# First attention: the softmax maxima stand ahead of the stick-breaking operations on VectorE

## The chip, the cores and the metric

The kernel runs on one core of one Trainium2 chip. The core has TensorE (PE, matmuls; its weight loads are shown as PEld), VectorE (DVE), ScalarE (ACT), GpSimd (POOL) and SyncE (SP, which here issues the DMAs). Each engine works through its own instructions in order, and they meet through semaphores. The metric is the time of one execution on the device in microseconds, given as the median of several runs; lower is better.

## The reference

Two transformer-like blocks run one behind the other on 256 tokens of width 1024. The first block begins with two kinds of attention side by side, eight heads each, whose results are normalised, joined and multiplied by `w_o`; then come a mixture of experts and the second block. Only the two attentions matter here (queries in blocks of 128):

```python
def stick_breaking_attention(q, k, v):           # width 64 a head
        z = einsum('bhqd,bshd->bhqs', qi, k) * scale
        strict = kpos[None, :] < qpos[:, None]
        log_fail = where(strict, log_sigmoid(-z), 0.0)
        later = cumsum(log_fail, axis=3, reverse=True) - log_fail
        a = where(strict, exp(log_sigmoid(z) + later), 0.0)
        return einsum('bhqs,bshd->bqhd', a, v)
...
def chunk_causal_softmax_attention(q, k, v):     # width 96 a head
        sc = einsum('bhqd,bshd->bhqs', qi, k) * scale
        allowed = kchunk[None, :] <= qchunk[:, None]     # chunks of 64
        p = softmax(where(allowed, sc, -inf), axis=-1)
        return einsum('bhqs,bshd->bqhd', p, v)
```

The softmax needs the maximum of each row of `sc` before its exponentials. The stick-breaking attention needs no maximum, but a softplus of z (an absolute value, an exponential and a logarithm) and a running sum over the keys.

## The kernel before

Head n of the stick-breaking attention and head n of the softmax attention are handled together, as one head n, in a pipeline of 12 rounds. `attention_rounds()` gives for round i the heads at each of five depths: `new` = i, `one` = i - 1, `two_` = i - 2, `three` = i - 3, `four` = i - 4, each only while it names a head from 0 to 7. TensorE, ScalarE and VectorE each walk over these rounds with code of their own, so the order on each engine is the order in which that code is written; no scheduler and no table of costs moves anything. All score tiles are 128 x 384: two blocks of queries against the keys that they may see.

TensorE, in this order in a round: of `three` the transposes of the softmax weights (pT, L914); of `new` the stick-breaking scores z (L893, L894); of `one` the sums over keys t (L900 to L902); of `new` the transposes of q and k (qkT, L929); of `one` the softmax scores s (L935, L936); then the products with the values, of `three` (stick-breaking) and of `four` (softmax) (L906, L907). Round 1 has nine extra matmuls (L841) ahead of t.

ScalarE: of `two_` the exponential of the stick-breaking weights (L1448) and the softmax exponentials with their row sums (L1455, twice), which wait for the negated maxima (semaphore `neg_max`); of `three` the copy of pT out of its bank (L1465); of `new` Abs, Exp and Ln on z (L1472, L1473, L1474) and the copy of qkT (L1477); then every second round copies of finished outputs (L1480, L1486).

VectorE: of `two_` the masked weights (L1999), the reciprocal of the row sums (L2002) and the scaling of the softmax weights (L2004, L2005, semaphore `probs`); of `one` the sum t plus log weight (L2009); of `new` three operations on z, which I call the stick-breaking operations: L2015, which waits for L1474 (semaphore `log_part`), L2017 (semaphore `fails`, for the sums t of the next round) and L2018, the last reader of z; of `one` the softmax maxima: L2022 writes -1e30 over the parts of s that are not allowed, L2023 and L2024 reduce, L2025 scales and raises `neg_max`.

The five products pT, z, t, qkT and s of a round go through four PSUM banks (`psr0` to `psr3`, `NB` = 4) in turn, in that order, by the list `GROUPS`. TensorE may start a product only when the last reader of the fourth product before it has signalled `bank_drained`. So pT waits for the last reader of z of the round before (L2018); z for L2009; t for L1477; qkT for L1455 of the same round; s for L1465 of the same round.

```python
def bank(name):
    b, u = use(g_at[0], NB)
    g_at[0] += 1
    if u:
        pe.wait_ge(bank_drained[b], u)
    return psr[b]
```

Of the kernel before, what the change touches and what calls it, by code (L numbers as in the profile page):

```python
# [29 lines left out]
ALU = mybir.AluOpType  # L30
# [5 lines left out]
AX = mybir.AxisListType  # L36

P = 128
# [7 lines left out]
QKD, NOPE, ROPE = 96, 64, 32  # L46
ATT = 3 * P
# [50 lines left out]
def attention_rounds():  # L98

    for i in range(H1 + 4):  # L100
        yield i, (i if i < H1 else None), (i - 1 if 1 <= i <= H1 else None), (i - 2 if 2 <= i < H1 + 2 else None),\
            (i - 3 if 3 <= i < H1 + 3 else None), (i - 4 if i >= 4 else None)
# [135 lines left out]
def bank_fills(name):  # L238

    n = GROUP_NO[name]  # L240
    return 1 + sum(g not in LAST_TILE for g in GROUPS[n % NB:n:NB])
# [19 lines left out]
def build(nc, d):  # L261

    with ExitStack() as ctx:
        def sb(name, shape, dt=F32):
            return ctx.enter_context(nc.sbuf_tensor(name, shape, dt))

        def sem(name):
            return ctx.enter_context(nc.semaphore(name))
# [31 lines left out]
        stat = sb("stat", [P, 2, 8])  # L300
# [154 lines left out]
        neg_max = sem("neg_max")  # L455
# [36 lines left out]
        def used(eng, n, it=None, per=0):  # L492

            eng.wait_ge(tile_used, at(it, per, split_no, n + 1))
# [30 lines left out]
        def full(eng, name):  # L525

            b = GROUP_NO[name] % NB
            if name in LAST_TILE:
                used(eng, LAST_TILE[name])
            else:  # L530
                eng.wait_ge(bank_full[b], bank_fills(name))
            return psr[b]

        def drains(ins, name):

            return ins.then_inc(bank_drained[GROUP_NO[name] % NB], 1)

        def drained(eng, name):

            b, u = use(GROUP_NO[name], NB)  # L540
            eng.wait_ge(bank_drained[b], u + 1)
# [11 lines left out]
        def sm(b, k):  # L553
            return stat[:, b, k:k + 1]
# [130 lines left out]
        def _(pe):  # L685
# [111 lines left out]
            def split_tokens(tiles, width, blocks):  # L797


                at_k, starts = 0, range(0)  # L800
                for n in tiles:
                    per = SLOT // width
                    if n == tiles[0]:
                        first = {}
                        for q, (out, bank_no, parts, tb) in enumerate(blocks):
                            first.setdefault(bank_no, q * per)
                        starts = first.values()
                    split_product(n, [(out, slice(j * width, (j + 1) * width),
                                       *(x_[:, tb * P:(tb + 1) * P] for x_ in parts(at_k + j)))
                                      for out, _, parts, tb in blocks for j in range(per)],  # L810
                                  starts if n == tiles[0] else (), weights_move=True)
                    at_k += per
# [999 lines left out]
        def _(dve):  # L1812
            V = nc.vector
            st = Steps(dve, dve_step)
            TT, TS, STT = V.tensor_tensor, V.tensor_scalar, V.scalar_tensor_tensor

            def norm(k, n=D, out=None):

                if k >= BY_LOGS:
                    dve.wait_ge(root, k + 1)  # L1820
                    return
                ps = full(dve, ("norm", k))
                if k in IN_BANK:
                    TS(ms[:, :], ps[:, 0:T], 1.0 / n, EPS, ALU.mult, ALU.add).then_inc(mean_made, 1)
                    dve.wait_ge(root, k + 1)
                    V.reciprocal(rinv[:, :], rms[:, :]).then_inc(inverted, 1)
                    dve.wait_ge(inverted, IN_BANK.index(k) + 1)
                    return
                drains(TS(ms[:, :], ps[:, 0:T], 1.0 / n, EPS, ALU.mult, ALU.add), ("norm", k))
                dve.wait_ge(root, k + 1)  # L1830
                st.do(V.reciprocal(rinv[:, :] if out is None else out, rms[:, :]))
# [162 lines left out]
            for i, new, one, two_, three, four in attention_rounds():  # L1994
                if two_ is not None:
                    dve.wait_ge(weights_in, two_ + 1)
                    if two_ >= 2:
                        dve.wait_ge(o_done, two_ - 1)
                    TT(two["pa"][:, two_ % 2, :], two["dd"][:, two_ % 2, :], mask, ALU.mult).then_inc(sb_probs, 1)  # L1999
                    b = two_ % 2  # L2000
                    drained(dve, ("s", two_))
                    st.do(V.reciprocal(stat[:, b, 6:8], stat[:, b, 4:6]))  # L2002
                    e = two["E"][:, b, :]
                    TS(e[:, 0:P], e[:, 0:P], sm(b, 6), None, ALU.mult)  # L2004
                    TS(e[:, P:ATT], e[:, P:ATT], sm(b, 7), None, ALU.mult).then_inc(probs, 1)  # L2005
                if one is not None:
                    ps = full(dve, ("t", one))
                    drained(dve, ("z", one))
                    drains(TT(two["la"][:, one % 2, :], ps[:, 0:ATT], two["dd"][:, one % 2, :], ALU.add), ("t", one))  # L2009
                if new is not None:  # L2010
                    b = new % 2
                    dve.wait_ge(log_part, new + 1)
                    ps = full(dve, ("z", new))
                    sp_ = two["sp"][:, b, :]
                    st.do(STT(out=sp_, in0=ps[:, 0:ATT], scalar=0.0, in1=two["az"][:, b, :],  # L2015
                              op0=ALU.max, op1=ALU.add))
                    TT(two["spm"][:, b, :], sp_, mask, ALU.mult).then_inc(fails, 1)  # L2017
                    drains(TT(two["dd"][:, b, :], ps[:, 0:ATT], sp_, ALU.subtract), ("z", new))  # L2018
                if one is not None:
                    b = one % 2  # L2020
                    ps = full(dve, ("s", one))
                    st.do(V.memset(ps[0:64, 0:ATT].rearrange("p (a c) -> p a c", a=6)[:, 1:6:4, :], -1e30))  # L2022
                    V.reduce_max(sm(b, 0), ps[:, 0:P], AX.X)  # L2023
                    st.do(V.reduce_max(sm(b, 1), ps[:, P:ATT], AX.X))  # L2024
                    TS(stat[:, b, 2:4], stat[:, b, 0:2], -QKD ** -0.5, None, ALU.mult).then_inc(neg_max, 1)  # L2025
            norm(3, 512)
            apply(sbT, mixed[:, 0:4, :], par("sb_out_norm"), 4, normed)
            norm(4, 512)
# [1 line left out]
            for c in range(4):  # L2030
                ps = full(dve, ("wo", c))
# [12 lines left out]
            for c in range(2):  # L2044
                ps = full(dve, ("pq", c))
# [153 lines left out]
            for q in range(4):  # L2199
                ps = full(dve, ("vt", q))  # L2200
# [38 lines left out]
            for i in range(2 * H2 + 1):  # L2239
                if i < 2 * H2:  # L2240
                    b = i % 2
                    for c in range(2):
                        ps = full(dve, ("s2", i, c))
# [3 lines left out]
                if i >= 1:  # L2247
                    n = i - 1
                    b = n % 2
# [13 lines left out]
            for p_ in range(3):  # L2263
                piece = slice(p_ * 512, (p_ + 1) * 512)
                ps = full(dve, ("rt2", p_))
# [3 lines left out]
            for c in range(4):  # L2269
                ps = full(dve, ("eo", c))  # L2270
# [150 lines left out]
            ps = full(dve, ("mean", 0))  # L2421
# [10 lines left out]
            for c in range(4):  # L2432
                ps = full(dve, ("pw2", c))
# [206 lines left out]
```

## Time and profile before

| what | us |
|---|---|
| median of 3 runs | 1791.12 (1788.84 to 1792.03) |
| profiled execution: first to last instruction (span) | 1787.1 |
| first attention, rounds 0 to 11 | about 97 to 147 of the span |
| first weight product behind it (L959) starts | 153.4 |
| TensorE busy over the span | 1696.0 (95%) |
| VectorE busy | 1108.2 (62%) |
| ScalarE busy | 925.4 (52%) |
| GpSimd busy | 757.3 (42%) |

The page gives the profiled execution's time as its span alone, 1787.1 us, 4.0 below the median of the runs. Start times in all views count from the start of the span. A row of a timeline gives the start and the time of one or of several merged instructions; in square brackets is the idle time of the engine just before and the instruction that ended it. Ends of matmuls are modelled. PEclk is TensorE's granted clock as a share of 2.4 GHz, so that 0.50 is its lower level of 1.2 GHz.

### The profile page before, as it was taken

What the parts mean: (1) busy time and instruction counts of PE and PEld (TensorE: products, weight loads), DVE (VectorE), ACT (ScalarE), POOL (GpSimd) and SP (SyncE); (2) the same over time, 40 slices, a digit from 0 to 9 for tenths busy, and PEclk for the clock granted to TensorE, in tenths of its full rate; (3) what the DMA queues carried; (4) which work ended last, traced back from release to release, by engine and by line L of the source; (5) the groups of instructions that cost most, each with busy time, mean ns of one, the idle gap of its engine ahead of it and who ended that gap; (6) DMA issues with size and microseconds to landing.
All of it is one profiled execution on the core that took longest, in us unless ns stands there. A gap on an engine that the chain in (4) does not pass through costs nothing.

```text
span 1787.1 us, 31571 instructions
## 1 busy us (share of the span) xinstructions
PE 1696.0 (95%) x10752; PEld 1496.8 (84%) x10752; DVE 1108.2 (62%) x1987; ACT 925.4 (52%) x1531; POOL 757.3 (42%) x409
## 2 busy tenths in 40 slices
PE   9988999999999877999999999988999999799998
PEld 8867999999888766888888879956899988589997
DVE  2674365922543598777888777353655569565555
ACT  4463555555555677455454555242555564345554
POOL 4410568887888899000000003400355655005553
PEclk8999999999999999999999999999999999999999
DMA  6302555555777500888888864301556644055553
GB/s 217 106 32 71 172 171 186 177 182 206 282 282 282 177 1 13 281 285 291 293 292 284 286 231 163 95 24 48 177 182 185 190 150 131 1 166 188 188 180 126
DMA packets 86334, 312.33 MB, mean 175 GB/s; under 512 B 9840, under 2 KB 9840, under 8 KB 86128
## 3 DMA queue, kind: packets, MB, share of 16 engines
q1 hardware_dynamic: 85968, 309.35, 51.7%
q0 software_dynamic: 288, 1.97, 0.3%
q8 instruction: 46, 0.75, 0.2%
q14 instruction: 32, 0.26, 0.0%
HBM read 310.23 MB, written 1.05 MB: 174 GB/s over the span
## 4 chain that ended last, share of the span: by engine, by line
PE 78%; DVE 7%; POOL 7%; ACT 4%; issue 4%; DVEq 1%; POOLq 0%; ACTq 0%
PE psr L1052 19%; PE psr L764 18%; PE psr L824 14%; PE psr L827 7%; PE acc_all L764 7%; POOL sq L2481 5%; PE psr L752 3%; PE psr L959 2%; PE psr L713 1%; POOL wl L512 1%; DVE wl L512 1%; DVE arena L2399 1%; ACT wh L503 1%; PE psr L862 1%; DVE sq L1848 1%
## 5 line engine op out<-in xcount | busy, mean ns | idle before, releaser
L512 POOL TENSOR_TENSOR wl<-ring,wh 128x1024 fp32r<-128x1024 f32 x264 | 641.8, 2432 | 646.8 <-ACT wh L503 640.7
L503 ACT ACTIVATE wh<-ring 128x1024 fp32r<-128x1024 f32 x458 | 482.6, 1054 | 304.7 <-PE psr L764 173.9
L824 PE MATMUL psr<-hb,wh 128*128 128x512 f32 x1152 | 289.5, 393 | 0.7 <-DVE hb L1863 0.7
L512 DVE TENSOR_TENSOR wl<-ring,wh 128x1024 fp32r<-128x1024 f32 x194 | 240.3, 1239 | 59.0 <-ACT wh L503 58.0
L1052 PE MATMUL psr<-wh,hb 128*128 128x512 f32 x1024 | 252.9, 389 | 1.9 <-DVE hb L2178 1.9
L764 PE MATMUL psr<-hb,wh 128*128 128x256 f32 x1776 | 238.3, 287 | 4.7 <-DVE hb L1860 2.8
L824 PEld LDWEIGHTS psr<-hb,wh 128*128 128x128 f32 x1152 | 206.9, 189 | 38.9 <-DVE hb L1863 2.2
L764 PEld LDWEIGHTS psr<-hb,wh 128*128 128x128 f32 x1776 | 225.1, 195 | 8.5 <-issue 3.2
L1052 PEld LDWEIGHTS psr<-wh,hb 128*128 128x128 f32 x1024 | 192.1, 188 | 41.9 <-issue 2.0
L827 PEld LDWEIGHTS psr<-hb,wl 128*128 128x128 f32 x1152 | 156.9, 190 | 13.5 <-DVE wl L512 1.7
L827 PE MATMUL psr<-hb,wl 128*128 128x256 f32 x1152 | 161.0, 283 | 1.0 <-DVE wl L512 0.8
L2486 POOL DMA_DIRECT2D arena<-in_consts x1 | 0.8, 754 | 360.4 <-DVE x L2202 360.4
L1598 ACT ACTIVATE hb<-arena 128x256 fp32r (+1 forms) x128 | 53.4, 418 | 174.1 <-PE psr L1052 171.9
L1052 PE MATMUL psr<-wl,hb 128*128 128x512 f32 x512 | 136.8, 389 | 0.0
L764 PE MATMUL psr<-hb,wl 128*128 128x256 f32 x888 | 125.6, 284 | 0.6 <-POOL wl L512 0.6
L2110 DVE SCALAR_TENSOR_TENSOR sq<-sq,acc_all 128x1024 f32<-128x1024 f32 x96 | 116.6, 1214 | 0.6
L764 PEld LDWEIGHTS psr<-hb,wl 128*128 128x128 f32 x888 | 115.3, 193 | 1.1 <-POOL wl L512 1.1
L1052 PEld LDWEIGHTS psr<-wl,hb 128*128 128x128 f32 x512 | 96.1, 188 | 20.0
L1036 PE MATMUL psr<-sq 128*128 128x128 f32 x512 | 73.5, 288 | 28.7 <-POOL sq L2481 25.5
L2481 POOL TENSOR_SCALAR sq<-cst,rT 128x128 f32<-128x128 f32 x128 | 99.1, 789 | 3.8 <-PE psr L1036 3.7
L1036 PEld LDWEIGHTS psr<-sq 128*128 128x128 f32 x512 | 63.3, 195 | 38.9 <-issue 38.9
L2343 DVE TENSOR_TENSOR fgl<-arena,fgh 128x256 fp32r<-128x256 f32 x40 | 81.3, 2033 | 21.2 <-ACT fgh L1741 21.2
(357 smaller groups left out, 2482.7 us busy)
## 6 DMA issues: line engine op xcount, KB each, us to landing
ring<-in_peer_u SPq DMA_DIRECT2D x128, 512.0 KB, 3.5
ring<-in_peer_v SPq DMA_DIRECT2D x128, 512.0 KB, 4.9
sq<-in_ada_w SPq DMA_DIRECT2D x96, 512.0 KB, 3.8
ring<-in_ffn_a SPq DMA_DIRECT2D x44, 512.0 KB, 3.9
ring<-in_ffn_b SPq DMA_DIRECT2D x44, 512.0 KB, 3.5
ring<-in_ffn_d SPq DMA_DIRECT2D x44, 512.0 KB, 3.5
ring<-in_pw SPq DMA_DIRECT2D x24, 512.0 KB, 3.6
ring<-in_w_in SPq DMA_DIRECT2D x18, 512.0 KB, 3.6
```

Of the source, the lines that this page charges most:

```text
L503: nc.scalar.activation(wh[:, q % 2, :], ring[:, s, :], ACT.Copy).then_inc(high_ready, 1)
L512: eng.tensor_tensor(wl[:, q % 2, :], ring[:, n % NS, :], wh[:, q % 2, :], ALU.subtract)\
L752: last = mm(ps[:, m * T:(m + 1) * T], w[:, k, :], src[:, k, :], start=(k == 0), stop=(k == KC - 1))
L764: return mm(out, w, a, start=start, stop=stop, skip_group_check=True)
L824: mm(ps[:, :], wh[:, b, chunk(k)], hb[:, k, :, :], start=(k == 0), stop=False, skip_group_check=True)
L827: last = mm(ps[:, 0:T], wl[:, b, chunk(k)], hh[:, k, :], start=False, stop=(k == KC - 1), skip_group_check=True)
L1036: last = mm(ps[:, g * P:(g + 1) * P], oneA[:, c % 2, g, :], oneB[:, c % 2, g, :], start=True, stop=True)
L1052: last = mm(sums[2 * tb + half][:, :], act_part[:, j, tb * P:(tb + 1) * P], weights[:, w, half * 512:(half + 1) * 512], start=start, stop= ...
L1598: A(hh[:, j % KC, :], part, ACT.Copy).then_inc(c_high, 1)
L2110: STT(out=w, in0=w, scalar=1.0, in1=c_rows[0], op0=ALU.mult, op1=ALU.mult, accum_out=ada[:, m, 0:1]).then_inc(ada_used, 1)
L2343: TT(fgl[:, f % 2, :], fg[:, f % 2, :], fgh[:, f % 2, :], ALU.subtract).then_inc(fg_low, 1)
L2481: ins = nc.gpsimd.tensor_scalar(oneA[:, c % 2, g, :], iota, rT[:, 0, t:t + 1], rT[:, 2, t:t + 1], ALU.is_equal, ALU.mult)
```

## The change

On VectorE, in each round, the four instructions of the softmax maxima of `one` are written ahead of the three stick-breaking operations of `new`, and behind L2009. Nothing else differs. In round 0 there is no `one` and in round 8 no `new`, so the order moves in rounds 1 to 7.

```diff
                     drained(dve, ("z", one))
                     drains(TT(two["la"][:, one % 2, :], ps[:, 0:ATT], two["dd"][:, one % 2, :], ALU.add), ("t", one))
+                if one is not None:
+                    b = one % 2
+                    ps = full(dve, ("s", one))
+                    st.do(V.memset(ps[0:64, 0:ATT].rearrange("p (a c) -> p a c", a=6)[:, 1:6:4, :], -1e30))
+                    V.reduce_max(sm(b, 0), ps[:, 0:P], AX.X)
+                    st.do(V.reduce_max(sm(b, 1), ps[:, P:ATT], AX.X))
+                    TS(stat[:, b, 2:4], stat[:, b, 0:2], -QKD ** -0.5, None, ALU.mult).then_inc(neg_max, 1)
                 if new is not None:
                     b = new % 2
                     dve.wait_ge(log_part, new + 1)
...
                     TT(two["spm"][:, b, :], sp_, mask, ALU.mult).then_inc(fails, 1)
                     drains(TT(two["dd"][:, b, :], ps[:, 0:ATT], sp_, ALU.subtract), ("z", new))
-                if one is not None:
-                    b = one % 2
...
```

VectorE, round 3 (a steady round), before. `psr` with its number is the bank, `stat` holds maxima and row sums, and each row ends with the semaphores it waits for:

```order
L2009 TENSOR_TENSOR arena<-psr1,arena 128x384 [waits bank_drained3,bank_full1]
L2015 SCALAR_TENSOR_TENSOR arena<-psr0,arena 128x384 [waits bank_full0,log_part]
L2017 TENSOR_TENSOR arena<-arena,cst 128x384 [waits dve_step]
L2018 TENSOR_TENSOR arena<-psr0,arena 128x384
L2022 MEMSET psr3 64x2x64 [waits bank_full3]
L2023 TENSOR_REDUCE stat<-psr3 128x1 [waits dve_step]
L2024 TENSOR_REDUCE stat<-psr3 128x1
L2025 TENSOR_SCALAR stat<-stat 128x2 [waits dve_step]
```

The same round in the changed kernel, whose line numbers differ (L2013 to L2016 are the maxima, L2022, L2024 and L2025 the stick-breaking operations):

```order
L2009 TENSOR_TENSOR arena<-psr1,arena 128x384 [waits bank_drained3,bank_full1]
L2013 MEMSET psr3 64x2x64 [waits bank_full3]
L2014 TENSOR_REDUCE stat<-psr3 128x1 [waits dve_step]
L2015 TENSOR_REDUCE stat<-psr3 128x1
L2016 TENSOR_SCALAR stat<-stat 128x2 [waits dve_step]
L2022 SCALAR_TENSOR_TENSOR arena<-psr0,arena 128x384 [waits bank_full0,log_part]
L2024 TENSOR_TENSOR arena<-arena,cst 128x384 [waits dve_step]
L2025 TENSOR_TENSOR arena<-psr0,arena 128x384
```

The wait for s (`bank_full3`) now stands ahead of the operations on z (`psr0`), the last of which signals that `psr0` is free.

TensorE, the same round and the first product of the next, in both kernels alike (pT in `psr3`, z in `psr0`, t in `psr1`, qkT in `psr2`, s in `psr3`, then pT of the next round in `psr0`):

```order
L914 MATMUL psr3<-cst,arena 128x128 [waits probs,bank_drained3]
L914 MATMUL psr3<-cst,arena 128x128 x2
L893 MATMUL psr0<-arena 128x256 [waits bank_drained0]
L894 MATMUL psr0<-arena 128x128
L900 MATMUL psr1<-arena,cst 128x256 [waits fails,bank_drained1]
L901 MATMUL psr1<-arena,cst 128x128
L902 MATMUL psr1<-arena,cst 128x128
L929 MATMUL psr2<-cst,arena 96x128 [waits bank_drained2]
L929 MATMUL psr2<-cst,arena 96x128 x3
L935 MATMUL psr3<-arena 128x128 [waits bank_drained1,bank_drained3]
L936 MATMUL psr3<-arena 128x256
...
L914 MATMUL psr0<-cst,arena 128x128 [waits probs,bank_drained0]
```

Nothing moved here; the last row shows that the transposes that open a round wait for the bank of the z before them.

VectorE, rounds 7 and 8, where the last head comes in. Before:

```order
L2015 SCALAR_TENSOR_TENSOR arena<-psr0,arena 128x384 [waits bank_full0,log_part]
L2017 TENSOR_TENSOR arena<-arena,cst 128x384 [waits dve_step]
L2018 TENSOR_TENSOR arena<-psr0,arena 128x384
L2022 MEMSET psr3 64x2x64 [waits bank_full3]
L2023 TENSOR_REDUCE stat<-psr3 128x1 [waits dve_step]
L2024 TENSOR_REDUCE stat<-psr3 128x1
L2025 TENSOR_SCALAR stat<-stat 128x2 [waits dve_step]
L1999 TENSOR_TENSOR arena<-arena,cst 128x384 [waits o_done,weights_in]
L2002 RECIPROCAL stat<-stat 128x2 [waits bank_drained3]
```

In the changed kernel:

```order
L2016 TENSOR_SCALAR stat<-stat 128x2 [waits dve_step]
L2022 SCALAR_TENSOR_TENSOR arena<-psr0,arena 128x384 [waits bank_full0,log_part]
L2024 TENSOR_TENSOR arena<-arena,cst 128x384 [waits dve_step]
L2025 TENSOR_TENSOR arena<-psr0,arena 128x384
L1999 TENSOR_TENSOR arena<-arena,cst 128x384 [waits o_done,weights_in]
L2002 RECIPROCAL stat<-stat 128x2 [waits bank_drained3]
L2004 TENSOR_SCALAR arena<-arena,stat 128x128 [waits dve_step]
L2005 TENSOR_SCALAR arena<-arena,stat 128x256
L2009 TENSOR_TENSOR arena<-psr1,arena 128x384 [waits bank_drained0,bank_full1]
```

Between the last operation on z of head 7 and the masked weights L1999 of head 6 the maxima of head 6 no longer stand.

## Rows read from the trace of the kernel before

**Rows 1.** Windows: stretch, length, busy us of PE PEld DVE ACT POOL, PEclk, DMA, GB/s

```profile
115.90:121.46 5.56, 4.80 (x33) 3.44 (x31) 4.28 (x12) 3.94 (x11) 0.00 (x0) 1.00 0.00 0
...
127.02:132.58 5.56, 5.51 (x25) 4.33 (x27) 4.28 (x12) 3.27 (x9) 0.00 (x0) 0.69 0.00 0
...
138.20:147.00 8.80, 6.18 (x48) 4.26 (x48) 4.75 (x17) 5.41 (x18) 0.00 (x0) 1.00 0.01 2
...
147.00:181.00 34.00, 31.50 (x144) 27.08 (x144) 11.45 (x19) 9.03 (x18) 0.00 (x0) 1.00 0.33 108
```

**Rows 2.** Timeline of VectorE, a steady round: start us, us, engine, line, operation

```profile
119.84 0.56 DVE L2015 SCALAR_TENSOR_TENSOR arena<-psr,arena 128x384 f32<-128x384 f32 x1 [0.45 <-ACT arena L1474]
...
120.91 0.55 DVE L2018 TENSOR_TENSOR arena<-psr,arena 128x384 f32<-128x384 f32 x1
121.48 0.17 DVE L2022 MEMSET psr<- 64x128 f32 x1
...
122.41 0.56 DVE L1999 TENSOR_TENSOR arena<-arena,cst 128x384 f32<-128x384 f32 x1
123.53 0.17 DVE L2002 RECIPROCAL stat<-stat 128x2 f32<-128x2 f32 x1 [0.56 <-ACT arena L1455]
...
124.20 0.55 DVE L2009 TENSOR_TENSOR arena<-psr,arena 128x384 f32<-128x384 f32 x1
125.40 0.56 DVE L2015 SCALAR_TENSOR_TENSOR arena<-psr,arena 128x384 f32<-128x384 f32 x1 [0.65 <-ACT arena L1474]
```

**Rows 3.** Timeline of ScalarE, the same round

```profile
122.58 0.37 ACT L1455 ACTIVATE arena<-psr,stat 128x128 f32<-128x128 f32 x1 [1.07 <-issue]
...
124.84 0.52 ACT L1474 ACTIVATE arena<-arena 128x384 f32<-128x384 f32 x1
```

**Rows 4.** Waits from 98 to 147: who for whom, us, times, longest

```profile
DVE arena L2015 <- ACT arena L1474: 5.4, 6, 3.1
PE psr L914 <- DVE arena L2018: 5.0, 4, 2.1
...
ACT arena L1455 <- DVE stat L2025: 4.2, 3, 1.9
```

**Rows 5.** Timeline of TensorE, from L914 to s in several rounds

```profile
110.38 0.55 PE L914 MATMUL psr<-cst,arena 128*128 128x128 f32 x3 [2.10 <-DVE arena L2018]
...
114.75 0.85 PE L936 MATMUL psr<-arena 96*128 96x256 f32 x2
...
121.51 0.55 PE L914 MATMUL psr<-cst,arena 128*128 128x128 f32 x3 [0.81 <-DVE arena L2018]
...
123.59 0.39 PE L902 MATMUL psr<-arena,cst 128*128 128x128 f32 x2
...
124.48 0.60 PE L936 MATMUL psr<-arena 96*128 96x256 f32 x2
...
127.07 0.55 PE L914 MATMUL psr<-cst,arena 128*128 128x128 f32 x3 [1.19 <-DVE arena L2018]
...
144.46 0.52 PE L914 MATMUL psr<-cst,arena 128*128 128x128 f32 x3 [1.96 <-DVE arena L2005]
```

**Rows 6.** Timelines of TensorE and VectorE, rounds 1 and 2

```profile
103.51 0.60 PE L936 MATMUL psr<-arena 96*128 96x256 f32 x2
105.19 0.70 PE L893 MATMUL psr<-arena 64*128 64x256 f32 x2 [1.08 <-DVE arena L2018]
...
107.68 0.60 PE L936 MATMUL psr<-arena 96*128 96x256 f32 x2
...
103.53 0.55 DVE L2015 SCALAR_TENSOR_TENSOR arena<-psr,arena 128x384 f32<-128x384 f32 x1
```

**Rows 7.** Timelines of VectorE and TensorE, rounds 7 and 8

```profile
137.65 0.55 DVE L2018 TENSOR_TENSOR arena<-psr,arena 128x384 f32<-128x384 f32 x1
...
139.74 0.60 PE L936 MATMUL psr<-arena 96*128 96x256 f32 x2
...
141.51 0.17 DVE L2022 MEMSET psr<- 64x128 f32 x1
```

More of the change, by code:

```diff
@@ L2018, in _ @@
                     drains(TT(two["dd"][:, b, :], ps[:, 0:ATT], sp_, ALU.subtract), ("z", new))
-                if one is not None:
-                    b = one % 2
[L2021 to L2025, printed above, removed]
             norm(3, 512)
```

## The prediction, made blind

> **What bounds the kernel now.** I read the granted clock and busy time by stretch first, then the timeline of each engine inside the first attention, then the waits there, and last the steady round piece by piece. Only the first attention (about 98 to 147 us of the span) is touched. Behind it a weight product of TensorE starts, with the DMA engines at a share of 0.33 [rows 1]. Nothing there runs ahead of the attention, so a microsecond lost or won in the attention moves the end by a microsecond.
>
> A steady round takes 5.56 us: L2015 starts at 119.84 and again at 125.40 [rows 2]. The wait view names what closes this circle: VectorE's L2015 waits for ScalarE's L1474, ScalarE's L1455 for VectorE's L2025 [rows 4]. In words: ScalarE runs the softmax exponentials of head one-before and then Abs, Exp, Ln of the new head, from 122.58 until L1474 ends at 124.84 + 0.52 = 125.36 [rows 3]. VectorE answers with L2015, L2017, L2018, 1.62 us from 119.84 to 120.91 + 0.55 = 121.46, and only then takes the maxima, which let ScalarE start again at 122.58 [rows 2, 3]. So the maxima are 1.12 us of this circle. That is the circle the edit opens.
>
> There is a second circle, hidden today. TensorE's first work in a round, the three transposes L914 into the bank that held the scores z, waits for L2018: its start at 121.51 comes 0.05 us behind the end of L2018 at 121.46, those at 110.38 and 127.07 are named as waits for L2018 too, and the wait view has four of them, 5.0 us [rows 2, 4, 5]. The softmax weights that the transposes also need were done earlier (L2005 stands ahead of L2009 in VectorE's order, and L2009 starts at 124.20), so the bank is what holds TensorE. Behind L914 stand, on the same in-order queue, the new z (L893), the sums t (L900 to L902), the transposes qkT (L929) and the scores s (L935, L936). With t0 the end of L2018, t is complete at 123.59 + 0.39 = 123.98, or t0 + 2.52, and s at 124.48 + 0.60 = 125.08, or t0 + 3.62 [rows 5]. Today VectorE reads s only after L2018 of the same round, and so never waits for it.
>
> **The change part by part.** Nothing is removed or added: four VectorE instructions for each of eight heads change places with three others, and no DMA, POOL or SP row is passed.
>
> Round 1. The maxima of head 0 now stand before L2015. s ends at 103.51 + 0.60 = 104.11, plus 0.04 to release (an estimate, from the 0.05 between L2018 and L914), plus the four instructions. Their cost is the step from the start of L2022 (121.48) to that of L1999 (122.41), 0.93 us [rows 2]. L2015 would start at 105.08 in place of 103.53 [rows 6]: 1.55 us later.
>
> Round 2. z waits for L2018 there (bank of the z before): it started at 105.19 and s ended at 107.68 + 0.60 = 108.28, 3.09 us later [rows 6]. After the change L2018 ends at 105.08 + 1.62 = 106.70, z starts at 106.75, s ends at 109.84, and with 0.04 + 0.93 + 1.62 L2018 ends at 112.43. Before, it ended at 110.33, which is 0.05 ahead of the L914 that waited for it and started at 110.38 [rows 5]. The delay is 2.10 us so far.
>
> Rounds 3 to 7. Each now takes the second circle: 0.05 to start L914, 3.57 to the end of s, 0.04 to release, 0.93 for the maxima, 1.62 for L2015 to L2018. That is 6.21 us. Before, the five rounds from 110.33 to 137.65 + 0.55 = 138.20 took 27.87, or 5.57 each [rows 6, 7]. Five times 0.64 is 3.2 us. ScalarE is no longer late here: z stands ahead of t on TensorE and so is complete before t0 + 2.52, the three instructions on it take 3 x 0.53 = 1.6 (L1474 is 0.52, [rows 3]), so L1474 ends before t0 + 4.1, ahead of the maxima's end at t0 + 4.6. Nor does L1455 hold anything: even where it starts today, 1.12 us into the round, it lets VectorE begin L2009 at 124.20, t0 + 2.74, and end it at t0 + 3.3, ahead of s at t0 + 3.6 [rows 2]. VectorE then stands idle until s; that wait takes the place of the one removed. Queued behind the maxima are L2015 to L2018, and behind these TensorE.
>
> TensorE's clock. In the round from 127.02 to 132.58 the granted clock was 0.69, a mix of 2.4 and 1.2 GHz, and in that from 115.90 it was full [rows 1]. The two L914 starts with idle time of 2.10 and 1.19 us before them opened slow rounds, the one with 0.81 did not, and one with 1.96 at 144.46 did not either, as the stretch from 138.20 shows 1.00 [rows 1, 5]. In the slow round L914 to s took 110.38 to 114.75 + 0.85 = 115.60, 5.22 us against 3.57 [rows 5]. Before, these 1.65 us lay beside the circle of ScalarE, which stayed the longer one. Now they are on the path. The idle time before each L914 becomes 6.21 - 4.37 = 1.84 us (4.37 from 121.51 to 127.07 - 1.19, [rows 5]), longer than 1.19 in every round. So slow rounds cost from 0 (none) to 5 times 1.65 = 8.3 us, with one in round 2 up to 9.9. A gain is excluded here, since the fast rounds are already at full clock. I take two, as in this trace: 3.3 us. Of the four long gaps two fell in slow rounds, which for five or six gaps gives two or three; I take the lower, since a slow round is itself busier.
>
> By the Trainium skill, "TensorE: Matmul & The Clock Gate", section "A second HAM failure mode: psum-queue depth-cycling", short TensorE pauses between groups that cycle through PSUM banks can make the clock swing between its levels; taken strictly it would have every round swing and the sum rise to about +12.
>
> The tail. Round 8 has no new head, so its order stays. But the maxima of head 6 no longer stand between L2018 of head 7 and the rest. Before, the maxima of head 7 started at 141.51, 3.31 us after L2018 ended; s was complete at 139.74 + 0.60 = 140.34 [rows 7]. ScalarE can run L1455 of head 6 while VectorE is still at L2015 to L2018, and without the wait for it, 0.56 us, VectorE's L1999 to L2009 take 124.20 - 122.41 - 0.56 = 1.23 us up to the start of L2009 [rows 2]; t is complete before s. So L2022 starts at t0 + 2.14 + 0.04, and 1.13 us are given back; where L1455 came as late as today it would be nothing. I take 1.1. From there to the weight product all stays as it was.
>
> The sum: 2.1 + 3.2 + 3.3 - 1.1 = +7.5 us on a profiled execution whose span is 1787.1. The median of the runs is 1791.12, 4.0 over that span, and I leave that distance. Forecast: 1798.6 us.
>
> **The rivals.**
> *Faster: TensorE is not held.* If L914 were in truth free by the weights and not by the bank, the maxima would only leave the first circle, 1.12 us in each of seven rounds: -7.8, or 1783.3 us. VectorE's busy time of 4.28 in a round of 5.56 would allow it [rows 1]. Against it stand the four waits of L914 for L2018, one seen to end 0.05 us behind it [rows 2, 4, 5], and the sums t: with 0.05 + 2.47 + 0.04 + 0.52 + 0.93 + 1.62 = 5.63 us even the way over L2009 and the maxima is as long as the old circle. It decides where L914 starts before L2018 ends. 4%.
>
> The Trainium skill, "Perfetto Trace Analysis", section "Matmuls", has independent groups rotate through PSUM banks so that draining one overlaps the matmuls of the next; where that held here this rival would be the outcome, but the four waits say that four banks don't reach for five groups in a round.
>
> *No change: the wait for s is shorter than its record.* The end of a matmul is modelled. If s were readable 0.6 us before its record ends, or if the delay were made up behind the attention, the result is 1790 to 1793. For the first speaks only that no wait for s is in this trace, so that its size rests on records of TensorE alone; seven rounds times 0.6 would cancel the 4.2 us of the second circle. Against the making up speaks that the product behind starts as soon as the attention's last results are there, with the DMA engines at 0.33 [rows 1]. 7%.
>
> *Slower, but full clock throughout.* The second circle without slow rounds: 2.1 + 3.2 - 1.1 = +4.2, 1795.3 us. 17%; it needs gaps of 1.84 us to leave the clock up six times.
>
> *Slower, every round slow.* 4.2 + 8.3 = +12.5, to +14.1 with round 2: 1803.6 to 1805.2. 15%.
>
> That the change doesn't do what it says is excluded by the order of VectorE's rows; what remains, the delay falling out otherwise, is in the 7%.
>
> **How the numbers follow.** The forecast (one to four slow rounds, two likeliest) has 57%: 1797.0 to 1801.9. The full clock case has 17%, all slow 15%, no change 7%, faster 4%. The range from 1794.3 to 1803.0 takes in the forecast, the full clock case with a microsecond for the median of runs, and leaves out the faster and the unchanged cases and most of the all-slow one, about 2 in 10. A measurement of this kernel can tell about 0.2%, 3.6 us, from no change. The full clock case at +4.2 lies just over that; a third of it, 6%, I count as same. So faster 0.04, same 0.13, slower 0.83.
>
> **What would show it.** In the profile after: VectorE's maxima wait for PE L936 in rounds 1 to 7, about 0.5 us each; L2015's old wait for ScalarE is gone (its wait for L1474 near nothing), and so is ScalarE's for the maxima; L914 waits for the last stick-breaking operation (L2025 in the new numbering) in every round with 1.5 to 1.9 us of idle time; the round is 6.2 us long, or 7.8 where the granted clock falls; the maxima of head 7 start 2.2 us after the last of these operations. The weight product L959 starts 4 to 12 us later than 153.4. I am wrong where the maxima start without a wait for s, where L914 starts earlier than the bank's last reader ends, or where the attention is longer and the span is not.

## The result: slower by 1.0%, and outside the range

| | before | changed |
|---|---|---|
| median, us | 1790.9 (4 runs) | 1808.63 (1805.35 to 1811.19, 4 runs) |
| span of the profiled execution | 1787.1 | 1809.3 |
| that execution's own time | not given beside the span | 1811.19 |
| start of L841 (round 1) to start of L959 | 98.98 to 153.42 = 54.4 | 100.41 to 172.64 = 72.2 |
| granted clock between these two | 0.94 | 0.79 |

The ratio is 1.0104, 95% interval 1.0088 to 1.0120: 17.7 us slower, where 7.5 was forecast. The median of the changed kernel lies 5.6 us above the upper end of the range. The whole loss lies in the attention: from L841 to L959 it takes 72.2 - 54.4 = 17.8 us longer, as much as the medians differ. What the two profiled executions differ beyond that, 22.2 - 17.8, lies ahead of the attention (1.4 us) and in the 1630 us behind it (3.0 us, 0.2%), and is no more than executions of one kernel differ: the four of the changed kernel spread over 5.8 us. The profiled execution of the changed kernel is the slowest of its four, so that its 17.8 us agree with the medians' 17.7 so closely is in part chance.

The waits of the changed kernel in the attention, in the form of [rows 4] (who waits for whom: us, times, longest; L2009 reads t, L2013 is the first of the maxima, L2025 the last reader of z):

```profile
DVE arena L2009 <- PE psr L902: 18.0, 8, 3.5
PEld psr L914 <- DVE arena L2025: 14.0, 6, 3.4
PE psr L914 <- DVE arena L2025: 12.0, 6, 2.7
DVE psr L2013 <- PE psr L936: 8.5, 8, 1.6
...
DVE arena L2022 <- ACT arena L1474: 3.1, 1, 3.1
...
ACT arena L1455 <- DVE stat L2016: 2.3, 2, 1.5
```

VectorE's wait for ScalarE's L1474 is left only where it was 3.1 us long at the start, and ScalarE's wait for the maxima fell from 4.2 us in three rounds to 2.3 in two. In their place VectorE waits for TensorE, and the transposes of TensorE wait for VectorE in all six rounds from 3 to 8: the second circle of the prediction now sets the pace. TensorE's idle time ahead of L914, by the timeline that answers to [rows 5]:

```profile
115.04 0.90 PE L914 MATMUL psr<-cst,arena 128*128 128x128 f32 x3 [2.71 <-DVE arena L2025]
...
123.82 0.90 PE L914 MATMUL psr<-cst,arena 128*128 128x128 f32 x3 [1.91 <-DVE arena L2025]
...
129.37 1.06 PE L936 MATMUL psr<-arena 96*128 96x256 f32 x2
...
133.14 0.55 PE L914 MATMUL psr<-cst,arena 128*128 128x128 f32 x3 [1.78 <-DVE arena L2025]
...
158.23 0.55 PE L914 MATMUL psr<-cst,arena 128*128 128x128 f32 x3 [1.90 <-DVE arena L2025]
```

From L914 to the end of s the round that starts at 123.82 took 129.37 + 1.06 - 123.82 = 6.61 us, against 3.57 at full clock and 5.22 in the slowest round shown of before. The windows, in the form of [rows 1], one for each round from 2 to 7 and one for round 8:

```profile
108.21:114.99 6.78, 4.08 (x18) 3.10 (x18) 4.09 (x13) 3.46 (x9) 0.00 (x0) 0.64 0.00 0
114.99:123.77 8.78, 6.86 (x25) 5.17 (x25) 4.10 (x13) 3.94 (x10) 0.00 (x0) 0.69 0.01 2
123.77:133.09 9.32, 7.54 (x29) 5.52 (x29) 4.10 (x13) 4.22 (x11) 0.00 (x0) 0.63 0.00 0
133.09:140.97 7.88, 5.99 (x29) 4.55 (x29) 4.10 (x13) 4.22 (x11) 0.00 (x0) 0.78 0.00 0
140.97:150.29 9.32, 7.47 (x29) 5.48 (x29) 4.09 (x13) 4.22 (x11) 0.00 (x0) 0.64 0.00 0
150.29:158.18 7.89, 5.99 (x29) 4.56 (x29) 4.10 (x13) 4.22 (x11) 0.00 (x0) 0.78 0.01 2
158.18:165.00 6.82, 5.55 (x44) 3.96 (x45) 3.87 (x13) 3.24 (x10) 0.00 (x0) 1.00 0.01 2
```

No round from 2 to 7 kept the full clock. Round 2 took 6.8 us, and from round 3 on the lengths swing between 7.9 and 9.3 us. VectorE and ScalarE did about the same work as before (from L841 to L959 37.0 and 37.4 us busy, before 37.9 and 36.1); what grew is TensorE's time for the same 255 matmul records, 52.5 us in place of 42.6.

### The profile page after: what moved, and what is told of

Same layout as the page of the kernel before. It is cut to its first block, busy times and chain, and to the rows that moved or that the text cites. A ratio compares the mean times of both kernels' runs of the same rounds, so it can differ in the third digit from the quotient of the medians.

```text
span 1809.3 us, 31571 instructions
## 1 busy us (share of the span) xinstructions
PE 1705.7 (94%) x10752; PEld 1501.8 (83%) x10752; DVE 1112.0 (61%) x1987; ACT 926.9 (51%) x1531; POOL 758.0 (42%) x409
## 4 chain that ended last, share of the span: by engine, by line
PE 78%; DVE 7%; POOL 6%; issue 4%; ACT 3%; DVEq 1%; DMA 0%; SPq 0%; POOLq 0%; ACTq 0%
PE psr L1052 19%; PE psr L764 17%; PE psr L824 14%; PE psr L827 7%; PE acc_all L764 7%; POOL sq L2481 5%; PE psr L752 3%; PE psr L959 2%; POOL wl L512 1%; DVE wl L512 1%; PE psr L862 1%; ACT wh L503 1%; PE psr L713 1%; DVE arena L2399 1%; DVE sq L1848 1%
```

## The experiments

Two questions stood open: is it TensorE's place in the circle that costs, or the maxima's place on VectorE; and why every round was slow where two had been taken. All kernels below compute everything the kernel before computes, and each was timed against it on the same chip, the last one in a single execution. None was timed beside the changed kernel, so a distance to that one is a difference of two comparisons.

**1. Filling the pauses.** Into the changed kernel go matmuls of ones, into a bank (`acc[0]`) that lies idle in this stage:

```diff
                     outputs(acc[3], lambda tb: vt[:, tb, four, :], two["PT"][:, four % 2, :], four).then_inc(mo_done, 1)
+                if 1 <= i <= 7:
+                    for _ in range(9 if i < 3 else 6):
+                        mm(acc[0][:, 0:P], ones, ones, start=True, stop=True)
```

> The changed kernel with extra matmuls of ones into an unused PSUM bank at the end of TensorE's rounds 1 to 7 (9 in rounds 1 and 2, 6 in rounds 3 to 7, about 0.25 us each), in time in which TensorE would wait for the last reader of z. Nothing of the computation changes. Theory (TensorE is in the circle, and its clock falls in the pauses that the change makes): the granted clock stays at 1.00 in nearly all rounds, the rounds shrink from 7.9 to 9.3 us to about 6.2, and the time is about 4 us over the kernel before (1795), some 13 below the changed kernel. Rival (the clock is a bystander, the longer round comes from waits between the engines): no gain, 1808 or more, since the extra matmuls only add work in front of the next round.

Measured: 1793.82 against 1788.44, ratio 1.0031 (1.0018 to 1.0043), +5.4 us, in place of the changed kernel's 17.7. More work on TensorE made the kernel some 12 us faster than the changed one (17.7 - 5.4). A steady round of it, TensorE's timeline (L953 are the added matmuls) and window:

```profile
122.53 0.55 PE L914 MATMUL psr<-cst,arena 128*128 128x128 f32 x3 [0.36 <-DVE arena L2028]
...
126.83 1.60 PE L953 MATMUL acc_all<-ones 128*128 128x128 f32 x12
```

```profile
122.50:128.75 6.25, 5.90 (x41) 4.68 (x41) 4.08 (x13) 4.13 (x11) 0.00 (x0) 1.00 0.01 3
```

The clock is 1.00 in all rounds, and L914 starts every 6.27 us (110.00, 116.27, 122.53 and so on), where the sum of the prediction had 6.21. It still waits for the last reader of z (L2028 here). So this is the second circle by itself, and the rest of the loss was the clock. From L841 to the first weight product the profiled execution takes 59.4 us (96.37 to 155.73), where the changed kernel took 72.2 and the kernel before 54.4: 4.9 us for the circle and 12.9 for the clock.

**2. The same in the kernel before**, with three added matmuls a round.

```diff
+                if 1 <= i <= 7:
+                    for _ in range(3):
+                        mm(acc[0][:, 0:P], ones, ones, start=True, stop=True)
```

> The kernel before with 3 such extra matmuls at the end of each of TensorE's rounds 1 to 7. Theory: in the kernel before TensorE is not in the circle that sets the round (5.56 us), so a full clock gains nothing there and 0.75 us of filling costs nothing: within 1.5 us of the kernel before, rounds of 5.56 us, and the granted clock full in more of them. Rival (the clock cost time before too): 1 to 3 us faster.

Measured: 1788.66 against 1788.44, ratio 1.0003 (0.9992 to 1.0013). Nothing, as expected. The round at 0.69 was as long as the full-clock round below it, 5.55 us:

```profile
111.60:117.15 5.55, 5.51 (x23) 4.33 (x24) 4.27 (x12) 3.72 (x10) 0.00 (x0) 0.69 0.00 0
...
128.55:134.10 5.55, 5.23 (x35) 4.01 (x35) 4.18 (x12) 4.01 (x12) 0.00 (x0) 1.00 0.00 0
```

So before the change a slow TensorE round cost nothing: it was hidden by the circle of ScalarE and VectorE. [rows 1] say the same, 5.56 us at 1.00 and at 0.69. The filling is no gain of its own. It isn't free in every round either: the one behind the slow round took 5.83 us (the maxima start at 117.17 and 123.00), and then 5.56 again.

**3. Two banks of its own for z**, in the changed kernel. `acc[0]` and `acc[2]`, in turn by head; z leaves the list of groups, and two semaphores `z_full` and `z_drained` stand for the bank's two. With z out of the list the other four products have a bank each, so their waits for banks change as well:

```diff
-        if new is not None:
-            g.append(("z", new))
...
-                ps = bank(("z", hd))
+                ps = acc[2 * (hd % 2)]
+                if hd >= 2:
+                    pe.wait_ge(z_drained, hd - 1)
...
-                    drains(TT(two["dd"][:, b, :], ps[:, 0:ATT], sp_, ALU.subtract), ("z", new))
+                    TT(two["dd"][:, b, :], ps[:, 0:ATT], sp_, ALU.subtract).then_inc(z_drained, 1)
```

> The changed kernel with the stick-breaking scores z in two PSUM banks of their own in turn (two that lie idle in this stage), so that neither the transposes that open a round nor the next z wait for the last reader of z. Nothing of the computation changes. Theory (the changed order loses only because TensorE is held by that bank): the second circle is gone, the maxima have left the first, and a round takes about 4.4 to 4.9 us: 3 to 7 us faster than the kernel before (1784 to 1788), some 22 below the changed kernel. Rival (the maxima in front cost by their place on VectorE, whatever the banks): 1795 to 1808.

Measured: 1780.72 against 1788.44, ratio 0.9956 (0.9940 to 0.9973): 7.7 us faster than the kernel before, a little more than the 3 to 7 expected. VectorE's timeline of one round (L2015 the first of the maxima, L2025 the first and L2028 the last operation on z), then TensorE's, then a window:

```profile
119.80 0.17 DVE L2015 MEMSET psr<- 64x128 f32 x1 [0.39 <-PE psr L937]
...
121.81 0.55 DVE L2028 TENSOR_TENSOR arena<-acc_all,arena 128x384 f32<-128x384 f32 x1
...
124.34 0.17 DVE L2015 MEMSET psr<- 64x128 f32 x1 [0.39 <-PE psr L937]
```

```profile
120.44 0.55 PE L915 MATMUL psr<-cst,arena 128*128 128x128 f32 x3
...
122.03 0.67 PE L901 MATMUL psr<-arena,cst 128*128 128x256 f32 x2 [0.20 <-DVE arena L2027]
```

```profile
117.70:122.30 4.60, 4.40 (x30) 3.33 (x30) 4.07 (x14) 3.89 (x12) 0.00 (x0) 1.00 0.00 0
```

The transposes (L915 here) start at 120.44, long before L2028 ends at 122.36, and without a wait. A round takes 124.34 - 119.80 = 4.54 us, 1.02 less than 5.56: what opening the first circle gives when the second doesn't hold it. In the profiled execution the attention up to the first weight product is 48.8 us long (96.41 to 145.20), 5.7 less than before; the rest of the 7.7 isn't in the part that the edit touches, and L841's start alone (L840 here) differs by more than that between these profiled executions, from 96.05 to 100.41, with the same code ahead of it. What closes the round now goes from L2027 over t, qkT and s to the maxima, with a pause of 0.20 us on TensorE. The clock stayed at 1.00.

**4. The same banks in the kernel before**, the same edit.

> The kernel before with the same two banks for z. Theory: its circle goes over ScalarE and VectorE and has no bank in it, so the round stays at 5.56 us and the time within 1.5 us of the kernel before. Rival (the banks alone give the gain of the run before): 3 to 7 us faster here too.

Measured: 1788.37 against 1788.44, ratio 0.9996 (0.9986 to 1.0006). The transposes start at 114.37, 119.94 and 125.50, without a wait and still 5.56 or 5.57 us apart. Banks alone: nothing. Order alone: 17.7 us slower. Both: 7.7 us faster. Neither part can be judged without the other.

**5 to 7. Shorter and longer pauses.** The filling of experiment 1 with other counts in rounds 3 to 7 (rounds 1 and 2 always 9): 3, then 1, then 0.

```diff
-                    for _ in range(9 if i < 3 else 6):
+                    for _ in range(9 if i < 3 else 3):
```

> The changed kernel with the extra matmuls of ones as in e1_after_fill in rounds 1 and 2 (9 each), but 3 in place of 6 in rounds 3 to 7, so that a pause of about 1.1 us is left ahead of each round in place of 0.36. Theory (the clock falls by the length of the pause, and a pause of 1.1 us is about where it begins): between e1_after_fill and the changed kernel, nearer to the first, 1794 to 1800, with none to three slow rounds. Rival (the clock needs the whole pause filled): 1800 to 1808.

Measured: 1792.6 against 1789.3, ratio 1.0020 (1.0008 to 1.0031), +3.3 us, 1.4 below the lower end expected. Pauses of 1.03 us, no slow round in the profiled execution.

> As e5_after_fill_half, with one extra matmul in place of 3 in rounds 3 to 7: a pause of 1.6 us is left ahead of each round, between the 1.03 at which no round was slow and the 1.84 at which every round was. Theory (the fall comes by the length of the pause, gradually: in some rounds and executions): between the two, 1795 to 1803, with runs that differ more among themselves than those of either neighbour. Rival (the fall begins right above 1 us): 1800 or more, as e6_after_fill_first. Other rival (it begins only near 1.8): 1793.

Measured: 1795.5 (1793.17 to 1801.14) against 1788.76, ratio 1.0048 (1.0030 to 1.0066), +6.7 us. The profiled execution, 1794.69, had pauses of 1.48 us and no slow round; the two slowest, 1801.14 and 1799.95, had mean granted clocks of 0.985 and 0.984 over the whole span, the two fastest, 1793.17 and 1793.45, had 0.989 and 0.990. That fits rounds that are slow in some executions and not in others, but it isn't shown: no slow one was profiled, and the kernel before, timed beside it, spread over 5.5 us itself with mean clocks from 0.986 to 0.990.

From L841 to the first weight product the profiled executions with 6, 3 and 1 added matmuls all take 59.4 us (96.37 to 155.73, 96.09 to 155.45, 99.35 to 158.72), though the pauses are 0.36, 1.03 and 1.48 us. As long as the clock stays full, the filling changes nothing.

> The changed kernel with the extra matmuls in rounds 1 and 2 alone (9 each); rounds 3 to 7 keep their pauses of about 1.85 us. Theory (each pause lets the clock fall by itself): as slow as the changed kernel less what round 2 lost, 1803 to 1807, with granted clocks of 0.6 to 0.8 in most rounds from 4 on. Rival (the two pauses of 2.7 us at the start bring the clock down and the slow rounds keep it there): the clock stays up and the time is that of e1_after_fill, about 1794.

Measured: 1802.04 (1799.82 to 1807.18) against 1789.3, ratio 1.0065 (1.0048 to 1.0082), +12.7 us by the medians and +11.6 by the ratio; 1 us better than the lower end expected. Its profiled execution, the slowest of four, took 70.3 us for the same stretch (100.14 to 170.39). L914 in these three kernels, with 3, 1 and 0 added:

```profile
122.25 0.55 PE L914 MATMUL psr<-cst,arena 128*128 128x128 f32 x3 [1.03 <-DVE arena L2028]
```

```profile
125.52 0.55 PE L914 MATMUL psr<-cst,arena 128*128 128x128 f32 x3 [1.48 <-DVE arena L2028]
```

```profile
120.06 0.88 PE L914 MATMUL psr<-cst,arena 128*128 128x128 f32 x3 [1.91 <-DVE arena L2028]
```

and two windows of the one with 0, the last round at full clock and the one after it:

```profile
113.75:120.01 6.26, 4.36 (x25) 3.23 (x25) 4.10 (x13) 3.86 (x10) 0.00 (x0) 1.00 0.00 0
120.01:129.30 9.29, 7.56 (x29) 5.50 (x29) 4.09 (x13) 4.22 (x11) 0.00 (x0) 0.63 0.00 0
```

The first unfilled pause, 1.91 us behind a round at full clock, was followed by a round of 9.29 us. The long pauses of rounds 1 and 2 are thus not needed for it, and the rival falls. Each matmul that is left out lengthens the pause and shrinks TensorE's work in the round, so these runs don't tell which of the two counts.

**8. TensorE's s ahead of t.** On top of experiment 3, TensorE's order z, qkT, s, t, and on VectorE the maxima ahead of the operation that reads t.

```diff
-                if one is not None:
-                    log_sums(one)
                 if new is not None:
                     if new == 0:
                         pe.wait_ge(qk_ready, 2)
...
                     fills(mm(ps[:, P:ATT], w[:, P:T], w[:, T:2 * T], start=True, stop=True), ("s", one))
+                    log_sums(one)
```

> e3_after_zbanks with TensorE's order z, qkT, s, t in place of z, t, qkT, s, and VectorE's maxima ahead of the operation that reads t, so that the scores s no longer stand behind the sums t, which wait for the second stick-breaking operation of the round before. Theory: VectorE's wait for s (0.39 us in each round of e3_after_zbanks) goes, and its own work of about 4.1 us sets the round: 4.2 to 4.3 in place of 4.54, 1 to 2 us faster than e3_after_zbanks. Rival (t comes later now, and VectorE waits for it in place of s): as e3_after_zbanks or slower.

Measured: 1778.89 against 1789.3, ratio 0.9939 (0.9923 to 0.9956), 10.4 us faster than the kernel before. The intervals of this and experiment 3 overlap, so the step between them rests on the rows: from L840 to the first weight product 45.6 us (99.04 to 144.63) in place of 48.8, 3.2 less where 1 to 2 were expected. The maxima start at 114.98 and again at 119.14, and VectorE waits for s in one steady round only, 0.17 us.

```profile
114.98 0.17 DVE L2010 MEMSET psr<- 64x128 f32 x1
...
119.14 0.17 DVE L2010 MEMSET psr<- 64x128 f32 x1
```

The round is 4.16 us (4.29 and 4.30 in two of them), and VectorE works through it without a wait. This version beats both kernels.

**9. One part of the change alone**, the maxima ahead of the operations on z in rounds 1 and 2 only, behind them from round 3 on.

```diff
-                if one is not None:
+                if one is not None and i in (1, 2):
...
+                if one is not None and i not in (1, 2):
...
```

> The maxima ahead of the stick-breaking operations in rounds 1 and 2 alone, behind them as before from round 3 on. One look, for the rows. Theory: the last operation on z of round 2 ends 2.1 us later than in the kernel before, counted from the start of TensorE's 18 extra rows of ones, or up to 3.3 with a fallen clock; round 3 then takes about 1.1 us less than 5.56, since the maxima it needs are there already, and the rounds after it 5.56 again. Rival (the moved order slows later rounds too): rounds 4 to 7 longer than 5.6.

One execution: 1792.4 us, which says little. By the rows, L914 of round 3 starts at 111.35, 15.30 us behind L841 at 96.05; before it was 110.38 - 98.98 = 11.40. That is 3.9 us later, more than the 3.3 expected; if 2.1 is the order, as forecast, 1.8 is left for the clock. Round 3 did not get shorter by 1.1: the first operation on z starts at 109.68 in round 2 and at 115.95 and 121.95 in rounds 3 and 4, that is after 6.27 and 6.00 us, with TensorE behind; then at 127.51, 133.07 and 138.63, every 5.56 us. Round 4 is thus longer than 5.6, as the rival had it, but with TensorE still late from round 3 and the order as before; from round 5 on no round is slowed, and there the rival falls. The expected gift in round 3 was eaten by the fallen clock: its transposes took 0.55 us, but the s of that round 1.06. To the first weight product it takes 59.4 us (96.05 to 155.46), 5.0 more than before: two rounds in the new order cost as much as all seven at full clock.

The rows of this run show something else. Pauses of 1.19 us stood ahead of rounds 6, 7 and 8, and the matmuls behind them ran at full clock; the kernel before had the same 1.19 ahead of a slow round [rows 5].

```profile
134.74 0.55 PE L914 MATMUL psr<-cst,arena 128*128 128x128 f32 x3 [1.19 <-DVE arena L2025]
...
137.70 0.60 PE L936 MATMUL psr<-arena 96*128 96x256 f32 x2
```

And where experiment 4 had 1.96 us ahead of the last transposes, the matmuls behind them were slow, 1.07 us for four; the kernel before had 1.96 there and full clock.

```profile
144.66 0.52 PE L915 MATMUL psr<-cst,arena 128*128 128x128 f32 x3 [1.96 <-DVE arena L2007]
145.11 1.07 PE L907 MATMUL acc_all<-arena 128*64 128x256 f32 x4
```

So the pause just ahead does not alone decide whether the clock falls.

## Why the prediction was wrong

The direction and the mechanism held; the size of one term, the slow clock, did not: 3.3 us were forecast for it and about 13 came. By its own steps:

*What bounds the kernel.* Right. The circle of ScalarE and VectorE was the bound, the bank of z held TensorE in a second one, and microseconds of the attention reached the end one for one. Experiments 3 and 4 show both circles: with the bank link cut the moved maxima gain 1.02 us a round, without the move the link costs nothing.

*Rounds 1 and 2, and the steady round.* L2022 of round 1 started at 106.59 - 100.41 = 6.18 us behind L841, against 103.53 - 98.98 = 4.55: 1.6 later, forecast 1.55. Of the steady round, 6.21 was forecast and 6.27 measured with the pauses filled. The sum without the clock, +4.2, stands against +5.4 (3.2 to 7.7) in experiment 1 and +3.3 (1.4 to 5.5) in experiment 5, and against +4.9 by the rows of both. Right within 0.7 us.

*The tail.* The maxima of head 7 start at 160.41, 2.23 us behind the end of L2025 at 158.18; forecast 2.18, before 3.31 [rows 7]. That step was right, 1.08 us given back. But "from there to the weight product all stays as it was" did not hold: L1999 behind these maxima waited 0.54 us for ScalarE's L1448, where before it started at once, and from L2025's end to L959 14.46 us passed against 15.22 before. Only 0.76 us reached the end.

```profile
158.09 0.55 DVE L1999 TENSOR_TENSOR arena<-arena,cst 128x384 f32<-128x384 f32 x1
...
160.41 0.17 DVE L2013 MEMSET psr<- 64x128 f32 x1 [0.16 <-PE psr L936]
...
161.97 0.56 DVE L1999 TENSOR_TENSOR arena<-arena,cst 128x384 f32<-128x384 f32 x1 [0.54 <-ACT arena L1448]
```

*TensorE's clock: the step that failed.* The prediction took "two, as in this trace: 3.3 us", from two slow rounds at 1.65 us each. Both factors were too small. How many: all six from 2 to 7. How much: a round's price is not 1.65. In the round of before from which that number came the clock fell only some way into the round: its L914 still took 0.55 us [rows 5]. In the changed kernel L914 took 0.90 in the slow rounds at 115.04 and 123.82, so these were slow from their first matmul; the second cost 9.32 - 6.21 = 3.1 us, one slow in part 7.88 - 6.21 = 1.7. Round 2 took 6.78 where 112.43 - 106.70 = 5.73 was forecast, 1.1 more, and round 3 had 8.78 - 6.21 = 2.6; with 3.1, 1.7, 3.1 and 1.7 that makes 13.3 us. Then 2.1 + 3.2 + 13.3 - 1.1 = 17.5, and with the 0.8 that the tail gave in place of 1.1 it is 17.8, as this execution's attention had it; the medians differ by 17.7. Against experiment 1 the clock's share is 72.2 - 59.4 = 12.9.

Why all six, where the prediction took the lower count because "a slow round is itself busier"? In the kernel before that held: the slow work ran into TensorE's own pause, and the next transposes started without one.

```profile
116.33 0.55 PE L914 MATMUL psr<-cst,arena 128*128 128x128 f32 x3
...
132.98 0.55 PE L914 MATMUL psr<-cst,arena 128*128 128x128 f32 x3
```

In the changed kernel a slow round pushes back s, the maxima and the last reader of z with it, so the pause behind it is still there: 1.91, 1.78, 1.90, 1.85 and 1.90 us ahead of rounds 4 to 8. The rows show the pauses; that they are what kept the clock from staying up is argued, with experiments 1 and 6 for it.

*The range.* Its bound for the clock, six times 1.65, was the price of a partly slow round taken for the highest price. A higher bound could be had from the same rows: at half the clock 3.57 us of TensorE work can become up to twice that, by estimate 3.6 us more for each round. And the four long gaps of before, two of them followed by a slow round, were read as a chance of one half for each, where they were pauses of different lengths and in different surroundings; with five or six pauses of 1.84 us in a row the case of all rounds slow deserved more than 15%.

*The cover that was named.* The prediction said that the slow clock lay beside the longer circle and would come onto the path; experiment 2 shows that it did cost nothing there, and the changed kernel that it now costs in full. The pauses came out as forecast, 1.78 to 1.91 us against 1.84.

*The rivals.* Faster by TensorE not being held: the bank did hold it, and experiment 3 is what this rival would have been. Its -7.7 beside the -7.8 that was priced is luck: the rows give -5.7 in the attention, 1.02 and not 1.12 in each steady round. No change: the wait for s is real, 8.5 us in eight rounds, and the median moved by 17.7. Full clock: experiment 1 had to make it. Every round slow was the right one, at 12.5 to 14.1 where 17.7 came.

Of the Trainium skill's two places, "TensorE: Matmul & The Clock Gate", section "A second HAM failure mode: psum-queue depth-cycling", which has the clock oscillate where TensorE pauses briefly between groups that cycle through PSUM banks (seen there in a bf16 kernel), was the better guide: the granted clock did swing, 0.63, 0.78, 0.64, 0.78 in the windows above. "Perfetto Trace Analysis", section "Matmuls", has matmul groups rotate through banks so that draining one overlaps the next; with two more banks that held, 120.44 against 122.36 in experiment 3.

## What to carry to other kernels

Before a step is moved out of one circle, look for the circles that run beside it: an engine that waits today for the last reader of a buffer, with its idle time covered, takes over as soon as anything is put ahead of that reader. Take that buffer out of the ring first, and then move the step; either edit alone showed nothing or a loss. And where an edit lengthens TensorE's pauses, take half the clock for the whole round as the upper bound for the matmuls on the path (here the rounds from 4 on paid 3.1 and 1.7 us in turn, of an estimated 3.6 at most), since in the rows of a kernel in which they are hidden the fall may be seen only in part.

## What the runs showed of the hardware

In the profiled executions of experiments 1 and 5, with pauses of TensorE of 0.36 and 1.03 us ahead of each steady round and 5.9 and 5.2 us of work in it, no round was slow. With 1.48 us the profiled execution had none either; two of the six executions were 6 to 8 us longer than the two fastest, at a lower mean clock, and whether their rounds were slow is open. With 1.74 to 1.91 us and 4.4 us of work at full clock (experiment 6) each of the five rounds behind such a pause was slow in the profiled execution, the first with 9.29 us behind one of 6.26. The pause alone doesn't fix it: 1.19 us stood ahead of a slow round in the kernel before and ahead of three at full clock in experiment 9, and 1.90 us ahead of round 8 of the changed kernel, at 158.23, was followed by full clock. Between its two levels, 1.2 and 2.4 GHz, the clock went down and up again within each pair of rounds. Work that computes nothing, 1.6 us in each steady round and 2.2 in the first two, was worth about 12 us.
